# Weight remainders on VectorE alone, in TensorE's order, in a two-block transformer kernel

## The reference

```python
# first block, two layers
z = rms_norm(x, norm_g[i]) @ w_in[i]                    # 1024 -> RWKV7, sparse and dilated branches
y = concatenate([rwkv7(z_a), dsa(z_b), dilated(z_c)])
x = x + y @ w_out[i]
gate = sigmoid(rms_norm(x, ple_norm_g[i]) @ ple_w_gate[i])
x = x + gate * (p[i] @ ple_w_proj[i])
...
# second block: an attention mixer, then w_o, then this, twice
def conv_ffn(h, w_up, conv_w, conv_b, w_down):          # D_FF = 2816
    u = h @ w_up                                        # 1024 -> 2 * 2816
    u = causal_depthwise_conv(u, conv_w) + conv_b       # width 3, over the tokens
    a, b = u[..., :D_FF], u[..., D_FF:]
    return (silu(a) * b) @ w_down
```

## Time and profile before

| | |
|---|---|
| median of three runs | 1552.84 us (1551.9 to 1553.16) |
| profiled execution | 1553.33 us, of which the span in the profile is 1551.4 |
| instructions | 25100 |
| TensorE busy | 1340.0 us, 86% of the span |
| VectorE busy | 897.6 us, 58% |
| ScalarE busy | 648.6 us, 42% |
| GpSimd busy | 495.3 us, 32% |
| remainders (L399) on VectorE | 162 instructions, 256.3 us |
| remainders (L399) on GpSimd | 163 instructions, 388.0 us |
| DMA | 167.56 MB, 108 GB/s, about 31% of the 16 DMA engines' time |

### The profile page before, as it was taken

How to read it: one execution, slowest core, us unless ns; L and a number is a source line. 1 busy time by engine, 2 the same in 40 slices (tenths; PEclk the granted TensorE clock), 3 DMA queues, 4 the chain that set the end, 5 groups by cost and what they waited for, 6 DMA issues and landing times.

```text
span 1551.4 us, 25100 instructions
## 1 busy us (share of the span) xinstructions
PE 1340.0 (86%) x10545; PEld 1223.1 (79%) x10545; DVE 897.6 (58%) x1579; ACT 648.6 (42%) x1144; POOL 495.3 (32%) x294
## 2 busy tenths in 40 slices
PE   3969885989698859879899899986988999999787
PEld 3957774988577749779777699885988878999787
DVE  1884647457746474557755446777436344588842
ACT  3533123465331235554532345454434333555541
POOL 1544100334440003346400224444545201344541
PEclk9989966999799659889855599998989856999989
DMA  6324100344330004326210144443534301444450
GB/s 242 133 102 141 56 2 1 114 159 136 109 131 29 2 1 169 130 82 234 73 55 1 44 147 136 136 154 131 182 132 139 132 1 55 139 161 163 153 179 35
DMA packets 24448, 167.56 MB, mean 108 GB/s; under 512 B 2704, under 2 KB 2832, under 8 KB 8336
## 3 DMA queue, kind: packets, MB, share of 16 engines
q1 hardware_dynamic: 24336, 165.96, 30.8%
HBM read 164.90 MB, written 1.05 MB: 107 GB/s over the span
## 4 chain that ended last, share of the span: by engine, by line
PE 37%; DVE 16%; ACT 7%; issue 2%; POOL 0%; DMA 0%; DVEq 0%; ACTq 0%; SPq 0%
PE ps L445 7%; PE ps L440 7%; PE ps L442 7%; DVE ARENA L2038 5%; PE ps L603 4%; PE ps L622 4%; DVE FR L399 3%; ACT FR L386 3%; DVE WL L399 2%; ACT WH L386 2%; PE ps L612 2%; DVE ARENA L2030 1%; PE ps L483 1%; PE ps L471 1%; PE ps L463 1%
## 5 line engine op out<-in xcount | busy, mean ns | idle before, releaser
L399 POOL TENSOR_TENSOR WL<-raw,WH 128x1024 fp32r<-128x1024 f32 (+3 forms) x105 | 246.6, 2349 | 385.4 <-ACT WH L386 385.3
L440 PE MATMUL ps<-FR,WH 128*128 128x256 f32 x1156 | 290.8, 290 | 43.4 <-ACT WH L386 28.8
L442 PE MATMUL ps<-FR,WH 128*128 128x256 f32 x1156 | 285.0, 285 | 2.3 <-DVE FR L504 1.3
L440 PEld LDWEIGHTS ps<-FR,WH 128*128 128x128 f32 x1156 | 222.5, 192 | 47.5 <-issue 31.9
L386 ACT ACTIVATE WH<-raw 128x1024 fp32r<-128x1024 f32 (+4 forms) x211 | 203.1, 984 | 132.6 <-PE ps L445 68.1
L399 DVE TENSOR_TENSOR WL<-raw,WH 128x1024 fp32r<-128x1024 f32 (+4 forms) x106 | 155.0, 1464 | 156.1 <-ACT WH L386 156.0
L440 PE MATMUL ps<-FR,FR 128*128 128x256 f32 x772 | 201.0, 296 | 30.1 <-ACT FR L508 22.9
L442 PEld LDWEIGHTS ps<-FR,WH 128*128 128x128 f32 x1156 | 222.5, 192 | 4.3 <-DVE FR L504 2.0
L442 PE MATMUL ps<-FR,FR 128*128 128x256 f32 x772 | 198.8, 292 | 4.3 <-DVE FR L512 3.7
L399 POOL TENSOR_TENSOR FR<-raw,FR 128x1024 fp32r<-128x1024 f32 (+2 forms) x58 | 141.4, 2441 | 137.7 <-ACT FR L386 137.7
L440 PEld LDWEIGHTS ps<-FR,FR 128*128 128x128 f32 x772 | 152.6, 198 | 35.5 <-ACT FR L508 21.5
(11 more groups left out here) (315 smaller groups left out, 2147.4 us busy)
## 6 DMA issues: line engine op xcount, KB each, us to landing
raw<-wst_in SPq DMA_DIRECT2D x123, 1024.0 KB, 4.9
raw<-wst_in SPq DMA_DIRECT2D x17, 896.0 KB, 4.6
raw<-wst_in SPq DMA_DIRECT2D x11, 768.0 KB, 4.3
raw<-wst_in SPq DMA_DIRECT2D x4, 912.0 KB, 4.6
cst<-cst_in SPq DMA_DIRECT2D x1, 1681.0 KB, 13.3
...
```

The lines of the kernel that those rows point to most:

```text
L399: e.tensor_tensor(lo[:, 0:cols], src, hi[:, 0:cols].bitcast(F32), SUB).then_inc(*put(LO[me], ("lo", i)))
L440: pe.matmul(out, hv[:, k, :], src.hi[:, c, :], start=k0 == 0 and k == ks[0], stop=False)
L442: pe.matmul(out, hv[:, k, :], src.lo[:, c, :], start=False, stop=False)
```

## The change

`split_lo` loses its engine argument and is VectorE's alone: every item's remainder runs there, at the places where VectorE's list already had its half of them, in the order of the items, with one semaphore. All calls of `split_lo` in GpSimd's functions go. Nothing else moves: slots, raw buffers, how far ahead the items run, the loads and ScalarE's and TensorE's lists are as before. GpSimd is left with the token shift's differences, some work of the layers and attentions, and silu(a) * b. 163 subtractions move: 137 of 128x1024, 12 of 128x768, 8 of 128x256, 4 of 128x912, and 2 of 128x584. The order lists number the changed kernel's lines: there L399 is L395, L2030 is L2012, L2038 is L2020, L512 is L508, L504 is L500, L1752, L1756 and L1759 are L1743, L1747 and L1750, L1483, L1488 and L1492 are L1479, L1484 and L1488.

```diff
-    nxt = {"A": 0, "V": 0, "G": 0}
-    LO = {"V": "split_lo_v", "G": "split_lo_g"}
-
-    def lo_engine(i):
-        return "V" if i % 2 == 0 else "G"
+    nxt = {"A": 0, "V": 0}
...
-    def split_lo(e, q, me, *event, ahead=None):
-
-        while nxt[me] < items_until(event, ahead):
-            i = nxt[me]
-            nxt[me] += 1
+    def split_lo(v, q, *event, ahead=None):
+
+        while nxt["V"] < items_until(event, ahead):
+            i = nxt["V"]
+            nxt["V"] += 1
             cols, split = known.plan[i][1:]
-            if not split or lo_engine(i) != me:
+            if not split:
                 continue
...
-            e.tensor_tensor(lo[:, 0:cols], src, hi[:, 0:cols].bitcast(F32), SUB).then_inc(*put(LO[me], ("lo", i)))
+            v.tensor_tensor(lo[:, 0:cols], src, hi[:, 0:cols].bitcast(F32), SUB).then_inc(*put("split_lo", ("lo", i)))
...
     def ffn_g(g_, q, l):
...
             if i < FC:
-                split_lo(g_, q, "G", "up", l, i)
                 if i == 0:
                     barrier(q, "G", ("P", l))
...
-        for c0 in range(0, 8, 2):
-            split_lo(g_, q, "G", "down", l, c0)
         B.mark("G", "end", ("F", l), "G")
```

More of the change, by code:

```diff
@@ L1471, in layer_v @@
                 c0 = 2 * s[1]
-                split_lo(v, q, "V", "cols", l, c0)
+                split_lo(v, q, "cols", l, c0)
                 if c0 == 0:
@@ L1511, in layer_v @@
                 g, k = s[1:]
-                split_lo(v, q, "V", "rows", l, g, k)
+                split_lo(v, q, "rows", l, g, k)
                 if (g, k) == (0, 0):
@@ L1678, in layer_g @@
                         part_lo(g_, q, "part_lo_g", p_parts[i], ("p", i), 0, m.PT[:, i, 0, :])
-            elif s[0] == "rows":
-                split_lo(g_, q, "G", "rows", l, *s[1:])
             elif s[0] in ("part dil", "part dsa"):
@@ L1773, in out_v @@
         for c0 in range(0, 8, 2):
-            split_lo(v, q, "V", "w_gate", l, c0)
-            split_lo(v, q, "V", "w_proj", l, c0)
+            split_lo(v, q, "w_gate", l, c0)
+            split_lo(v, q, "w_proj", l, c0)
             gate_pair_v(v, q, l, c0)
@@ L1843, in out_g @@
         barrier(q, "G", ("L", l))
-        for c0 in range(0, 8, 2):
-            split_lo(g_, q, "G", "w_out", l, c0)
-        for c0 in range(0, 8, 2):
-            split_lo(g_, q, "G", "w_gate", l, c0)
-            split_lo(g_, q, "G", "w_proj", l, c0)
         if l == 1:
@@ L1896, in between_v @@
                 .then_inc(*put("scaled", ("x fin", c), *([("mean free", ("in", 2))] if c == 7 else [])))
-        split_lo(v, q, "V", "mem k", 0)
-        split_lo(v, q, "V", "mem v", 0)
+        split_lo(v, q, "mem k", 0)
+        split_lo(v, q, "mem v", 0)
         B.mark("V", "end", "T", "V")
@@ L1952, in o_v @@
         barrier(q, "V", stage)
-        split_lo(v, q, "V", "w_o", l, 0, ahead=5)
+        split_lo(v, q, "w_o", l, 0, ahead=5)
         for c in range(8):
@@ L1957, in o_v @@
         for c0 in range(0, 8, 2):
-            split_lo(v, q, "V", "w_o", l, c0)
+            split_lo(v, q, "w_o", l, c0)
             ps, free = psum("w_o", l, c0)
@@ L1986, in o_g @@
     def o_g(g_, q, l):
-        for c0 in range(0, 8, 2):
-            split_lo(g_, q, "G", "w_o", l, c0)
         B.mark("G", "end", ("P", l), "G")
@@ L2023, in ffn_v @@
             if i < FC:
-                split_lo(v, q, "V", "up", l, i)
+                split_lo(v, q, "up", l, i)
                 if i == 0:
@@ L2045, in ffn_v @@
         for c0 in range(0, 8, 2):
-            split_lo(v, q, "V", "down", l, c0)
+            split_lo(v, q, "down", l, c0)
             ps, free = psum("down", l, c0)
@@ L2278, in nsa_v @@
         barrier(q, "V", "T")
-        split_lo(v, q, "V", "mem k", 1)
+        split_lo(v, q, "mem k", 1)
         rstd_v(v, q, ("fin", 1), None, m.zt[:, 0, 0:256])
         scaled_v(v, q, X, vcol("attn_norm_2", 0, 0, 8), m.H, "HN", m.hs, ("fin", 1), mean_bank[:, 0:S])
-        split_lo(v, q, "V", "mem v", 1)
+        split_lo(v, q, "mem v", 1)
         def group(g):
-            split_lo(v, q, "V", "nrows", g)
+            split_lo(v, q, "nrows", g)
             dst = m.zt[:, 1, 512 * g:512 * g + NSA_N[g]] if g < 2 else m.zv[:, 1, :]
@@ L2296, in nsa_v @@
         for c0 in range(0, 6, 2):
-            split_lo(v, q, "V", "zc", c0)
+            split_lo(v, q, "zc", c0)
         for x in range(2):
@@ L2336, in compress_v @@
             if n < 2:
-                split_lo(v, q, "V", "cmp1", x, n)
+                split_lo(v, q, "cmp1", x, n)
             else:
@@ L2477, in nsa_g @@
         barrier(q, "G", "T")
-        split_lo(g_, q, "G", "mem k", 1)
         scaled_g(g_, q, m.H, "HN", m.hs)
-        split_lo(g_, q, "G", "mem v", 1)
-        split_lo(g_, q, "G", "nrows", 0)
-        split_lo(g_, q, "G", "nrows", 1)
-        for c0 in range(0, 6, 2):
-            split_lo(g_, q, "G", "zc", c0)
         fl = lambda x: x.rearrange("p v l n -> p (v l n)")
@@ L2487, in nsa_g @@
         g_.tensor_tensor(fl(m.Ul), fl(m.U), fl(m.Uh).bitcast(F32), SUB).then_inc(*put("cmp_g", ("Ul",)))
-        split_lo(g_, q, "G", "nrows", 2)
         for x, s in m.steps:
-            if x == "compress":
-                if s < 6 and s % 3 < 2:
-                    split_lo(g_, q, "G", "cmp1", s // 3, s % 3)
-            elif x not in (0, 1):
+            if x not in ("compress", 0, 1):
                 attn_g(g_, q, x, s)
@@ L2563, in fox_v @@
         barrier(q, "V", ("F", 0))
-        split_lo(v, q, "V", "forget")
+        split_lo(v, q, "forget")
         rstd_v(v, q, ("f", 0), None, m.OT[:, 0, 0:256])
@@ L2571, in fox_v @@
         for c0 in range(0, 6, 2):
-            split_lo(v, q, "V", "k pe", c0)
+            split_lo(v, q, "k pe", c0)
             ps, free = psum("k", c0)
@@ L2597, in fox_v @@
         for g in range(2):
-            split_lo(v, q, "V", "v pe", g)
+            split_lo(v, q, "v pe", g)
             ps, free = psum("v", g, 1)
@@ L2611, in fox_v @@
         for c0 in range(0, 8, 2):
-            split_lo(v, q, "V", "q pe", c0)
+            split_lo(v, q, "q pe", c0)
         for x, s in m.steps:
@@ L2651, in fox_g @@
         barrier(q, "G", ("F", 0))
-        split_lo(g_, q, "G", "forget")
         scaled_g(g_, q, m.HK, "HK", m.hs)
-        for c0 in range(0, 6, 2):
-            split_lo(g_, q, "G", "k pe", c0)
         scaled_g(g_, q, m.H, "HX", m.hs)
-        for g in range(2):
-            split_lo(g_, q, "G", "v pe", g)
-        for c0 in range(0, 8, 2):
-            split_lo(g_, q, "G", "q pe", c0)
         B.mark("G", "end", "X", "G")
```

9 lines of the change are left out of this document (2 added, 7 removed), and 2 rows, old and new, of the table SEMS.

## The result

The changed kernel takes 1514.88 us (median of four, 1511.76 to 1517.03) where the kernel before took 1552.37 in the same rounds (1551.65 to 1553.16): a ratio of 0.9757, 95% interval 0.9737 to 0.9777, or 37.5 us less. The forecast was 1518.4, 34.4 less; both medians lie in its range of 1506 to 1535. The profiled execution took 1516.22, span 1514.3.

A forecast was written before the change was run, and what follows sets the result against it. The prediction took both `up` loops to be bound by the loop through VectorE, which waits for whole GpSimd instructions. Its terms, -23.6 - 7.0 - 6 + 4.6 - 0.9 - 1.5 = -34.4, took 1552.84 to 1518.4 us, range 1506 to 1535.

The forecast's parts named there:

- The price of the exclusion: VectorE's two-input operations and GpSimd's wait for each other by whole instructions; free remainders take 1.23 us, taps 1.78.
- F0 -23.6, F1 -7.0: Both feed-forwards' `up` loops: the period falls to 6.10 us a chunk, from 7.22 in F0 and 6.43 in F1.
- The parity argument: F0 and F1 `up` loops differ by 0.8 us a chunk only through which item of the pair VectorE has.
- What is won in `up` is kept: `down` follows at TensorE's pace, busy 25 of 25 us, so the gain of `up` stays; `down` itself 0.
- The layers' chains, -3 each: L0 and L1: VectorE's list reaches the last L1492 earlier, -3 us each, -6 together, bounds -10 and +2.
- Output stages, +4.6: O0 and O1: the last remainder stands ahead of L1752, +1.14 us per pair at most; half counted, bounds 0 and +9.
- Start, -0.9: Four L504 at the start are no longer stretched by GpSimd's first remainder: -0.9 us, bounds 0 and -1.3.
- N and X, -1.5: Mixer N and attention X: blocks on VectorE go, about as many remainders come; -1.5 us together, bounds -5 and +5.
- A: Rival: steps in the `up` loops overlap better, period some 5.9 us, total 1510; chance 7%.
- B: Rival: `up` gains, but VectorE's in-order list delays TensorE in layers, O, N and X; 1537 us, chance 12%.
- C: Rival: long F0 remainders belong to the place (loads, ScalarE reading), not GpSimd; slower, 1608 us, chance 6%.
- D: Rival: nothing happens, the loops are held by something else such as loads; 1552 us, chance 5%.

The follow-up runs named there:

- E6: Changed kernel plus an extra GpSimd subtraction of constant tables, read by nobody, at each odd item's rounding in the `up` loops: 1606.65 us.
- E7: Changed kernel plus two GpSimd memsets, which read nothing, at each odd item's rounding in the `up` loops: 1511.0 us.
- E1: Kernel before with only the feed-forwards' remainders (w_up, w_down) all on VectorE, others split as before: 1519.89 us, ratio 0.9786.
- E4: The full change measured again, unaltered, beside the other runs, against the kernel before: 1512.35 us, ratio 0.9743.
- E5: Kernel before with the engines exchanged, odd items' remainders on VectorE and even ones on GpSimd: 1573.57 us, ratio 1.0144.
- E2: Kernel before with all remainders except the feed-forwards' on VectorE, the feed-forwards split as before: 1544.38 us, ratio 0.9951.
- E9: Changed kernel with the taps of chunk i-1 ahead of the remainders on VectorE in the `up` loops: 1549.85 us, ratio 0.9986.
- E11: Changed kernel with taps ahead of remainders, silu(a) * b on VectorE, and gate and projection remainders split as before: 1499.41 us, ratio 0.9662.
- E8: Kernel before with both items' remainders of each feed-forward pair on GpSimd: 1555.23 us.

## Why the prediction was right

**The price of the exclusion: right.** In both loops the remainders take 1.22 to 1.23 us each and the taps 1.78. That GpSimd's work is the cause was argued in the prediction from rows 2 to 4, and is shown by E6 and E7.

**F0 -23.6, F1 -7.0: right.** Measured -23.8 and -7.6, in E1, E4 and the first profile alike to 0.1. The period of 6.10 was right in each of its links. The parity argument ("by nothing but which of the pair VectorE has") is shown by E5.

**What is won in `up` is kept: right.** `down` changes by 0.3 at most.

**The layers' chains, -3 each: right.** In L0 -2.3 and -3.0 in the two executions. In L1 the stage has -3.4 and -5.4, but to the matmul that ends the chain (at 410.64 before) it is -3.5 in both; the other 2 us come behind it, with the clock. "Five remainders" more counts from 66 us on; in all of L0 up to that matmul VectorE does 20 instead of 10. The Trainium skill (Perfetto Trace Analysis, Optimizing Scalar/DVE Operations) says that work of a saturated VectorE may be moved to another engine, GpSimd too, and doubts that this helps between VectorE and GpSimd. The trace agrees with the doubt: VectorE's list, on which TensorE waits, ended 2.6 us earlier with all the remainders on it than with half of them. TensorE's wait before the chain's end is 0.9 shorter (it was 13.27), not 10 as I wrote, since TensorE also reached it 1.8 earlier (100.02 - 12.38 against 102.66 - 13.27):

```profile
100.02 1.51 PE L942 MATMUL ps<-cst,ARENA 128*128 128x128 f32 x6 [12.38 <-DVE ARENA L1488]
```

**Output stages, +4.6: the size came out, in part by luck.** Gate and projection cost 3.1 in O0 and 1.4 in O1 in E4. The term was half of a bound, eight pairs by one remainder. In O0 only the first two slips (0.33 and 1.01) are that remainder; the third is a remainder of L1 in the same place, which I hadn't named, and 0.7 are the clock's. The first profile reads 3.9 and 3.1, in O0 with 2.5 of it in the 40 matmuls behind the gap, where the clock was 0.50.

**Start, -0.9: the wait went, and its gain is hidden by the clock.** TensorE's tenth matmul waited for L504 before, and doesn't in any kernel with VectorE's new list (the kernel before, then the changed one):

```profile
26.21 0.58 PE L442 MATMUL ps<-FR,WH 128*128 128x256 f32 x1 [0.90 <-DVE FR L504]
```

```profile
25.36 0.58 PE L438 MATMUL ps<-FR,WH 128*128 128x256 f32 x1
```

Yet TensorE is only 0.3 ahead at 48 us, 0.5 behind at 67 and 0.6 ahead at 71. In between lie a clock that rose to its higher level at 30.6 us in the profile of the kernel before and at 32.4 in that of the changed one (E1, with the old arrangement, was late as well and lost 1.0 by it), and a wait before 66 us that is 1.40 where it was 0.63. What of the 0.9 reaches the end of the layer stays open.

**N and X, -1.5: N read -3.0, -3.8 and, in E2, 0.0**, with the same remainders on the same engines in all three. Two us of this are one stretch of N in which the engines do the same work and the clock rises earlier or later. The kernel before, E4 and E2, each from the matmul that starts at 844.0 in the kernel before to the one at 847.8:

```profile
844.00:847.80 3.80, 3.80 (x12) 2.80 (x11) 1.71 (x5) 1.25 (x5) 0.00 (x0) 0.50 0.01 2
```

```profile
837.00:839.00 2.00, 2.00 (x11) 1.57 (x10) 1.48 (x4) 1.26 (x5) 0.00 (x0) 1.00 0.00 0
```

```profile
835.50:839.30 3.80, 3.80 (x12) 2.81 (x11) 1.70 (x5) 1.25 (x5) 0.00 (x0) 0.50 0.00 0
```

Of the nine kernels with all of N's remainders on VectorE six show the early rise and three (E2, E9, E11) don't; nor do E1 and E8, which have N as before. X, together with F0's `down` and P1, came to 0.0 and +0.2. What is left of N's part is between 0 and -2, and open.

**Mis-sized:** the sum was 34.4, the two sets of rounds gave 37.5 and 40.0. The feed-forwards account for 31.4 of it (forecast 30.6). The other 6 to 9 lie in the stages before, where the terms came to 3.8 and E2 measured 7.9. In E4's profile, which is 10.4 faster in these stages and so 6.6 more than the terms, 5.9 lie in four stretches with the same matmuls at a higher clock: 1.3 behind L1's chain (mean clock 0.93 against 0.87), 0.8 in L1 at 474 us (0.86 against 0.74), 1.7 in the memory projections (0.98 against 0.86) and 2.1 in N. The prediction had no term for the clock. Whether the change makes the higher clock more frequent isn't shown; in each of these places some of the changed kernels have it and others don't.

**Rivals.** A (5.9 a chunk) did not occur: 6.08 to 6.10. B (VectorE's list costs elsewhere) is real in O0 and O1, and 0.8 at one wait of L0. C is excluded by E6 and E7. D fell with the result.
